# The last output chunk multiplied tile by tile, its first token tile scored and routed behind the second

## The reference: one block of a hybrid network with a mixture of experts

```python
h = rmsnorm(x, norm1_g)
u = h @ w_in
x = x + concatenate([y_a, y_b, y_c]) @ w_out          # the "mixed" rows y, 256 x 2048
h = rmsnorm(x, norm2_g)
pg = softmax(h @ rg_w + rg_b);  grp = argmax(pg)       # 4 groups
le = (h @ re_w + re_b)[experts of grp]                 # 8 experts a group
q, e = top_k(softmax(le), 2)                           # 2 experts a token
x = x + sum over the 2 experts of gate * (silu(h @ w_gate[e]) * (h @ w_up[e])) @ w_down[e]
out = rmsnorm(x, final_g)
```

## The kernel before

| tensor | before | multiple of 64? | after | multiple of 64? |
|---|---|---|---|---|
| `y_hi`, `y_lo` (stationary, output projection) | 193248, 209632 | no, 32 over | 193152, 209536 | yes |
| `h_both` (stationary in `rows()` for the values, moving in `channels()`) | 23488 | yes | 23552 | yes |
| `w_hi0`, `w_lo0` | 89024, 113600 | yes | 89088, 113664 | yes |
| `x_parts`, `pick` (sort) | 138176, 17536 | yes | 138240, 17536 | yes |
| `sorted_rows` | 193248 | no, 32 over | 193152 | yes |
| `iota_row`, `ones_b` | 189568, 191744 | yes | 189472, 191648 | no, 32 over |

## Time and profile before

### The profile page before, as it was taken

One profiled execution on the slowest core, in us unless ns is written; L12 is line 12 of the kernel. 1 busy time (PEld: TensorE's weight loads), 2 busy tenths in 40 slices (PEclk: granted clock), 3 DMA queues, 4 the chain that ended last, 5 costly groups with the idle time before them and its releaser, 6 DMA issues.

```text
span 1338.6 us, 15622 instructions
## 1 busy us (share of the span) xinstructions
PE 1237.3 (92%) x5882; PEld 645.0 (48%) x5882; DVE 555.5 (41%) x977; ACT 284.2 (21%) x390; POOL 6.0 (0%) x27
## 2 busy tenths in 40 slices
PE   5999999999999999999999898898989898998995
PEld 4888888888884333333333333333333333333332
DVE  5476888775555332323232222322322232232234
ACT  5343444464432001100010000001000000100002
POOL 1000000000000000000000000000000000000000
PEclk9999999999989999999999999999999999999998
DMA  7655455447468999999999999999999999999995
GB/s 270 214 175 198 143 182 179 163 157 301 170 251 333 424 427 427 428 428 429 428 428 429 429 428 428 429 428 428 429 428 427 429 429 428 428 429 428 423 423 238
DMA packets 65168, 471.74 MB, mean 352 GB/s; under 512 B 6087, under 2 KB 6599, under 8 KB 37868
## 3 DMA queue, kind: packets, MB, share of 16 engines
q1 hardware_dynamic: 65132, 471.24, 86.2%
HBM read 469.13 MB, written 2.10 MB: 352 GB/s over the span
## 4 chain that ended last, share of the span: by engine, by line
PE 58%; DMA 35%; DVE 3%; issue 2%; ACT 1%; SPq 0%; DVEq 0%; ACTq 0%
DMA ring<-in_w_up 29%; PE bank L1600 19%; PE bank L1403 10%; PE bank L1417 8%; PE bank L1635 7%; DMA zone_u<-in_w_up 5%; PE bank L1648 4%; PE bank L1418 4%; PE bank L1570 1%; PE bank L1601 1%; DVE zone_u L920 1%; PE bank L1529 1%; PE bank L1421 1%; DMA x_tok<-in_x 1%; ACT gatesT L787 0%
## 5 line engine op out<-in xcount | busy, mean ns | idle before, releaser
L1600 PE MATMUL bank<-ring,win 128*64 128x512 f32 x816 | 375.0, 614 | 46.2 <-DMA ring<-in_w_up 32.1
L1601 PE MATMUL bank<-ring,win 128*64 128x512 f32 x816 | 372.5, 610 | 0.0
L1600 PEld LDWEIGHTS bank<-ring,win 128*64 128x64 f32 x816 | 111.6, 141 | 289.1 <-issue 267.9
L1417 PE MATMUL bank<-h_both,w_hi 128*128 128x512 f32 x540 | 193.4, 400 | 0.3 <-DVE w_lo L383 0.3
L1251 DVE SCALAR_TENSOR_TENSOR x_tok<-bank,gate_of,x_tok 128x512 f32<-128x512 f32 x256 | 174.4, 744 | 25.0 <-PE bank L1648 24.0
L1635 PE MATMUL bank<-ring,hiddenT 128*64 128x512 f32 x704 | 157.6, 600 | 13.2 <-ACT gatesT L787 12.7
L383 DVE TENSOR_TENSOR w_lo<-stage,w_hi 128x2048 fp32r<-128x2048 f32 x60 | 137.4, 2296 | 74.9 <-ACT w_hi L377 74.9
L1418 PE MATMUL bank<-h_both,w_lo 128*128 128x256 f32 x540 | 151.8, 281 | 0.0
L377 ACT ACTIVATE w_hi<-stage 128x2048 fp32r<-128x2048 f32 x60 | 115.0, 1918 | 132.6 <-PE bank L1418 84.9
L779 ACT ACTIVATE rows_now<-bank,root_row 64x512 f32<-64x512 f32 x32 | 21.8, 680 | 566.6 <-PE bank L1601 566.6
L1648 PE MATMUL bank<-y_rows,gatesT 64*128 64x512 f32 x512 | 126.9, 615 | 1.0 <-DVE y_rows L1275 1.0
(11 more groups left out here) (239 smaller groups left out, 1014.0 us busy)
## 6 DMA issues: line engine op xcount, KB each, us to landing
ring<-in_w_gate SPq DMA_DIRECT2D x49, 2048.0 KB, 35.2
ring<-in_w_up SPq DMA_DIRECT2D x48, 2048.0 KB, 31.9
ring<-in_w_down SPq DMA_DIRECT2D x40, 2048.0 KB, 31.9
stage<-in_w_in SPq DMA_DIRECT2D x44, 1024.0 KB, 5.1
zone_u<-in_w_down SPq DMA_DIRECT2D x19, 2048.0 KB, 31.9
zone_u<-in_w_up SPq DMA_DIRECT2D x9, 2048.0 KB, 34.1
zone_u<-in_w_gate SPq DMA_DIRECT2D x9, 2048.0 KB, 35.4
stage<-in_w_out SPq DMA_DIRECT2D x16, 1024.0 KB, 5.0
```

The lines of the kernel that those rows point to most:

```text
L1417: M.matmul(banks[j][:, :], hi[:, at], both, start=(c == 0), stop=False)
L1600: M.matmul(bank[0][0:W_ROWS, :], rows_of[:, c, 0:W_ROWS], gate[:, at], start=(c == 0), stop=(c == C - 1))
L1601: ins = M.matmul(bank[0][UPPER, :], rows_of[:, c, 0:W_ROWS], up[:, at], start=(c == 0), stop=(c == C - 1))
```

## The change

Four things are changed. (a) In the last chunk of the last output block PE makes the twelve products of token tile 0 first and then those of tile 1, and signals tile 0 by a semaphore of its own (`mixed_first`); VectorE adds tile 0 at once, and PE turns tile 0 between the products of tile 1 (`by_tile`). (b) Tile 0 is scored right behind the products, then tile 1 is turned and scored; the transposes of tile 1 go half to bank 5, half to bank 4, and ScalarE and VectorE copy one half each. Mean, root and its inverse are made for each tile alone. (c) The routing steps are written for one tile each, and tile 0's stand before or between those of tile 1. A tile has two casts and one comparison less: the mask takes the index as it is and is added in the same instruction, and `index` holds the two choices side by side (`[P, T, 2, 33]`), so that PE makes twelve instead of six products for the places and four instead of two for the sums; KEEP_ROUTE falls from 30 to 20. (d) `root_of` and `masked` change places in memory, `below` goes and `root_row` is padded to 24 floats, which moves every tensor behind them (table above).

The diff, cut to its core (removed routing steps, which the list above shows, are left out):

```diff
-KEEP_ROUTE, KEEP_PICK = 30, 24
+KEEP_ROUTE, KEEP_PICK = 20, 24
...
-        masked = sb("masked", [P, T, E])
+        root_of = sb("root_of", [P, T, E + OVER])
...
-        below = sb("below", [P, T, E + 1])
-        index = sb("index", [P, T, E + 1], BF16)
+        index = sb("index", [P, T, 2, E + 1], BF16)
...
-        root_of = sb("root_of", [P, T, E + OVER])
-        root_row = sb("root_row", [P, 1])
+        masked = sb("masked", [P, T, E])
+        root_row = sb("root_row", [P, 24])[:, 0:1]
...
+            def root_of_tile(t):
+
+                act.wait_ge(mean_sq, 1 + t + 1)
+                nc.scalar.activation(RT_[:, t:t + 1], MS[:, t:t + 1], ACT.Sqrt).then_inc(root, 1)
+
             rows_hi(BLOCKS - 1, 0)
+            root_of_tile(0)
             turned_out(BLOCKS - 1)
             squares(BLOCKS - 1, 1)
-            act.wait_ge(mean_sq, 2)
-            nc.scalar.activation(RT_, MS, ACT.Sqrt).then_inc(root, 1)
+            act.wait_ge(x_turned, T * (BLOCKS - 1) + 2)
+            nc.scalar.activation(xT[:, 1, 0:NB // 2], bank[5][:, 0:NB // 2], ACT.Copy).then_inc(xT_half, 1)
+            root_of_tile(1)
             rows_hi(BLOCKS - 1, 1)
...
+            def add_tile(b, t):
+
+                at = x_tok[:, t, b * NB:(b + 1) * NB]
+                V.tensor_tensor(at, at, bank[MIXED_BANK[b % 2] + t][:, :], ALU.add).then_inc(mixed_added, 1)
...
-            add_mixed(BLOCKS - 1)
...
-            dve.wait_ge(sq_made, T * (BLOCKS - 2) + 1)
-            dve.wait_ge(mixed_added, T * (BLOCKS - 1) + 1)
-            last = x_tok[:, 0, (BLOCKS - 1) * NB:]
-            squared = did(V.scalar_tensor_tensor(sq_out[0], last, 1.0, last, ALU.mult, ALU.mult,
-                                                 accum_out=sq_parts[:, 0, BLOCKS - 1:BLOCKS]))
-            turned_out(BLOCKS - 1)
-            dve.wait_ge(sq_made, T * BLOCKS - 1)
-            after(squared)
-            after(did(V.tensor_reduce(SS, sq_parts[:, :, :], AX.X, ALU.add)))
-            V.tensor_scalar(MS, SS, 1.0 / D, EPS, ALU.mult, ALU.add).then_inc(mean_sq, 1)
-            dve.wait_ge(root, 2)
-            V.reciprocal(RSTD, RT_).then_inc(h_ready, 1)
-            dve.wait_ge(h_ready, T + 1)
...
+            def mean_of_tile(t):
+
+                after(did(V.tensor_reduce(SS[:, t:t + 1], sq_parts[:, t, :], AX.X, ALU.add)))
+                V.tensor_scalar(MS[:, t:t + 1], SS[:, t:t + 1], 1.0 / D, EPS, ALU.mult, ALU.add).then_inc(mean_sq, 1)
+
+            def root_of_tile(t):
+
+                dve.wait_ge(root, 1 + t + 1)
+                V.reciprocal(RSTD[:, t:t + 1], RT_[:, t:t + 1]).then_inc(h_ready, 1)
+
+            def logits_of(t):
+
+                dve.wait_ge(h_ready, T + t + 1)
+                dve.wait_ge(scored, T * LAST + t + 1)
+                return did(V.scalar_tensor_tensor(lg[:, t, :], bank[6 + t][:, 0:RW], RSTD[:, t:t + 1], rbias[:, :],
+                                                  ALU.mult, ALU.add))
...
+            def other_group(t):
+                return did(V.tensor_tensor(masked[:, t, :], grp_of[:, :], gidx[:, t, 0:1].broadcast_to([P, E]), ALU.not_equal))
+
+            def mask_others(t):
+                return did(V.scalar_tensor_tensor(masked[:, t, :], masked[:, t, :], MASKED, lg[:, t, GW:], ALU.mult, ALU.add))
...
+            def mark_later(t):
+
+                every = iota_row[:, 0:E + 1].unsqueeze(1).broadcast_to([P, 2, E + 1])
+                V.tensor_tensor(index[:, t, :, :], every, eidx[:, t, 0:2].unsqueeze(2).broadcast_to([P, 2, E + 1]),
+                                ALU.is_gt).then_inc(index_ready, 1)
...
+            dve.wait_ge(mixed_first, 1)
+            add_tile(LAST, 0)
+            dve.wait_ge(sq_made, T * (LAST - 1) + 1)
+            dve.wait_ge(mixed_added, T * LAST + 1)
+            last = x_tok[:, 0, LAST * NB:]
+            after(did(V.scalar_tensor_tensor(sq_out[0], last, 1.0, last, ALU.mult, ALU.mult, accum_out=sq_parts[:, 0, LAST:])))
+            mean_of_tile(0)
+            rows_lo(LAST, 0)
+            root_of_tile(0)
+            dve.wait_ge(used, chunk(4 * (OUT_BLOCK0 + LAST) + 3))
+            add_tile(LAST, 1)
...
+            a0 = logits_of(0)
+            dve.wait_ge(sq_made, T * BLOCKS - 1)
+            mean_of_tile(1)
+            after(a0)
+            a0 = group_max(0)
+            dve.wait_ge(x_turned, T * LAST + 3)
+            V.tensor_copy(xT[:, 1, NB // 2:], bank[4][:, NB // 2:]).then_inc(xT_dve, 1)
+            after(a0)
+            a0 = group_index(0)
+            root_of_tile(1)
+            after(a0)
+            a0 = other_group(0)
+            after(a0)
+            a0 = mask_others(0)
+            after(a0)
+            a0 = expert_max(0)
+            a1 = logits_of(1)
+            after(a1)
+            a1 = group_max(1)
+            a0 = expert_index(0)
+            after(a1)
+            a1 = group_index(1)
+            after(a1)
+            a1 = other_group(1)
+            mark_later(0)
+            after(a1)
+            a1 = mask_others(1)
+            after(a1)
+            a1 = expert_max(1)
+            after(a1)
+            a1 = expert_index(1)
+            after(a1)
+            mark_later(1)
...
+            chosen = did(V.tensor_copy(CHOICE.rearrange("p (t k) -> p t k", t=T), eidx[:, :, 0:2]))
...
-            rows_lo(BLOCKS - 1, 0)
+            after(chosen)
...
-            def rows(b, br, banks, left_hi, left_lo, before_chunk=None):
...
+                    if by_tile is None or m < STAGES - 1:
+                        order = [(i, t) for i in range(CM) for t in range(T)]
+                    else:
+                        order = [(i, t) for t in range(T) for i in range(CM)]
+                    for i, t in order:
+                        c, at, tt = m * CM + i, slice(i * NB, (i + 1) * NB), slice(t * P, (t + 1) * P)
+                        ins = products(banks[t][:, :], ((left_hi[:, c, tt], hi[:, at]), (left_hi[:, c, tt], lo[:, at]),
+                                                        (left_lo[:, c, tt], hi[:, at])), c == 0, c == C - 1)
+                        if by_tile is not None and m == STAGES - 1:
+                            by_tile(i, t, ins)
...
+            def turn_tile(b, t):
+
+                x_j = x_tok[:, t, b * NB:(b + 1) * NB].rearrange("p (k j) -> p j k", j=J)
+                pe.wait_ge(mixed_added, T * b + t + 1)
+                for j in range(J):
+                    other = b == BLOCKS - 1 and t == T - 1 and j >= 2
+                    ins = M.transpose(bank[4 if other else 4 + t][:, j * P:(j + 1) * P], x_j[:, j, :], ident[:, :])
+                    if b == BLOCKS - 1 and t == T - 1 and j == 1:
+                        ins.then_inc(x_turned, 1)
+                ins.then_inc(x_turned, 1)
...
+            def score_tile(b, t):
                 pe.wait_ge(rw_ready, RW_STEPS)
-                for t in range(T):
+                if b == BLOCKS - 1 and t == T - 1:
+                    pe.wait_ge(xT_half, 1)
+                else:
                     pe.wait_ge(xT_dve if t else xT_act, b + 1)
-                    for j in range(J):
-                        ins = M.matmul(bank[6 + t][:, 0:RW], xT[:, t, j * P:(j + 1) * P], rw[:, b * J + j, :],
-                                       start=(b == 0 and j == 0), stop=(b == BLOCKS - 1 and j == J - 1))
-                    ins.then_inc(scored, 1)
+                for j in range(J):
+                    if b == BLOCKS - 1 and t == T - 1 and j == 2:
+                        pe.wait_ge(xT_dve, b + 1)
+                    ins = M.matmul(bank[6 + t][:, 0:RW], xT[:, t, j * P:(j + 1) * P], rw[:, b * J + j, :],
+                                   start=(b == 0 and j == 0), stop=(b == BLOCKS - 1 and j == J - 1))
+                ins.then_inc(scored, 1)
...
+            def first_tile_out(i, t, ins):
+
+                if t == 0 and i == CM - 1:
+                    ins.then_inc(mixed_first, 1)
+                if t == 1 and i == 1:
+                    turn_tile(BLOCKS - 1, 0)
...
-            turn_block(BLOCKS - 1)
-            score_block(BLOCKS - 1)
+                rows(b, b % 3, bank[at:at + 2], yT_hi, yT_lo, former_block if i else mixers_done,
+                     first_tile_out if i == BLOCKS - 1 else None)
+
+            score_tile(BLOCKS - 1, 0)
+            turn_tile(BLOCKS - 1, 1)
+            score_tile(BLOCKS - 1, 1)
...
-                later = index[:, t, 1:]
-                M.matmul(dst, before_b[:, :], later, start=True, stop=False)
-                M.matmul(dst, from_b[:, :], index[:, t, 0:E], start=False, stop=False)
-                other = index[:, 1, 0:E] if t == 0 else index[:, 0, 1:]
-                M.matmul(dst, ones_b[:, :], other, start=False, stop=True).then_inc(places_done, 1)
+                for k in range(2):
+                    M.matmul(dst, before_b[:, :], index[:, t, k, 1:], start=(k == 0), stop=False)
+                    M.matmul(dst, from_b[:, :], index[:, t, k, 0:E], start=False, stop=False)
```

(22 more changed lines are left out.)

63 lines of the change are left out of this document (16 added, 47 removed).

## The result

| | before | after |
|---|---|---|
| median, us | 1338.49 (1337.86 to 1338.9) | 1329.69 (1329.44 to 1330.13, 4 runs) |
| ratio to before | | 0.9932, 95% interval 0.992 to 0.9944 |
| the profiled execution, its span | 1340.45, 1338.6 | 1329.68, 1327.9 |

The direction was right, 3.6 us of gain were not foreseen, and the two terms of the sum did not come out alike: the tail won 3.4 us in the profile where 2.8 were forecast, the products 0.4 where 2.4 were.

The account below looks back on a forecast made before the run. The kernel was taken as bound by a DMA transfer of fixed length whose start PE's progress to the sort sets. 2.4 (spacing) + 2.8 (tail) = 5.2 us won, giving 1333.3 us, range 1330.9 to 1336.2.

Parts of the forecast that it names:

- the tail: Last output block up to the sort: reordered tiles and shorter routing steps win 2.8 us, bounds 1.4 and 3.9.
- the products: Output projection: operand starts at a multiple of 64 bytes bring 384 products from 233 to 227 ns, 2.4 us.
- The full stream: Expert loads, 414.60 to 1320.60 us: fixed length, 906 us at DMA share 1.00; only its start can move.
- Rival 1: Output projection: spacing stays at 233 ns, operand start not the cause, only 2.8 won; 1335.7 us, chance 0.25.
- rival 3: All PE stages: spacing depends on operands' places to each other, channels() and values lose; 1341.0 us, chance 0.06.
- rival 4: All PE stages: same dependence the other way, all reach the short spacing, 4.1 us more; 1329.2 us, chance 0.07.
- P: End of all products of the last block before the change, 387.12 us, from which later times are counted.
- the working at the full clock: Last products to sort: 2.1 + 0.68 + 0.5 = 3.3 us won, sort at P + 7.95 instead of P + 11.24.
- us to spare: Last chunk: VectorE's 3.1 us on tile 0 fit within 3.3 us of tile 1's products, 0.2 to spare.
- logits of tile 1: Routing after the last block: VectorE has them within 3.1 us of the last product.
- the DMA's pause: Ahead of the sort's first half piece: the 3.1 us gap closes, no gap of over 1 us left.
- The 0.5 charged for the clock: Between last products and sort: 0.5 us taken off the 3.3 won, in case PE's waits lower the clock.

Follow-up runs that it names:

- the last but one experiment: Kernel before with 224 bytes of padding ahead of pos, so y_hi and w_hi starts differ by a multiple of 256; 1336.5 us, ratio 0.9978.
- the table of pairs: Kernel of products alone, no loads or reference work, 20 series with both operands' starts varied modulo 256; 226.7 to 234.3 ns a product.
- the kernel without fillers: Kernel after with KEEP_ROUTE and KEEP_PICK at 0, leaving out 44 products that nobody reads; 1332.29 us, ratio 0.9953.

## Why the prediction was wrong

**The full stream.** This is the step that failed: "a transfer of fixed length, and no engine can shorten it. What can move is its start", and for the profile after "906 us at a DMA share of 1.00 unchanged". The change moves the ring from 23488 to 23552, and the stream's length depends on that: 6.6 us in the profile, 5.3 to 7.1 in the profiles of three other pairs of kernels and 6.3 to 7.5 in their medians. The table of starts showed the new place of `h_both`, and `ring0` begins where `h_both` does; I asked of each start only what it does to PE. A DMA share of 1.00 says that the queue is never empty, not that each packet is as short as it can be: between 420 and 1300 us a packet of 16 KB took 615.1 ns in the mean before and 611.3 after (the medians, 613 and 611, show only half of this). The Trainium skill had the rule that asks for this: "DMA: Bandwidth & Descriptors", section "How a descriptor splits into AXI transactions", says that a transfer that does not start at a multiple of 256 bytes begins its first transaction at the boundary below and pays for the bytes it does not use. It is written of reads; the runs here show that a multiple of 256 counts at the side where the ring is written. Its account of the cost does not fit them: an estimate from that page, 65 transactions for 64 in a row of 16 KB, is 1.6%, two to three times the 0.5 to 0.7% measured, and with the bytes before the start as the cost 32 over would be the cheapest of the places off the multiple, where it was the slowest (428.1 GB/s). So the runs show the condition, and the mechanism behind it stays open.

**The spacing of the products.** The step said of the values' and the output's products that "the two differ in little else" than in whether the start is a multiple of 64, and took 2.4 us between bounds of 0 and 2.4. Measured: 0.4. The size was right for an operand well placed (2.3 in the last but one experiment), but the multiple of 64 is not the condition. Before, `y_hi` stood 32 from `w_hi` modulo 256, the values' operand 0, and `x_parts` 64 from `pick`. After, they stand at 128, 0 and 128. Measured are 233.3, 226.8 and 233.3 ns before and 232.4, 226.8 and 232.4 after, each within 0.2 of what the table of pairs has for that distance. The sort's 233 ns, named as evidence against and then set aside, was the row to follow: an aligned operand with the long spacing refuted the condition. Rival 1 had the size of this term and rival 3 its cause ("their places to each other"); `channels()` and the values lost nothing, and there both operands moved by the same 64 bytes. That rival 4's time, 1329.2, lies within 0.5 us of the measured one is chance: the shorter stages on which it rests did not come, and `channels()` kept its 159.6 us.

**The tail.** Right. The sort starts at 7.81 us behind the end of the products of this stage, counted without the transposes as P was, where the working at the full clock had 7.95. Its parts hold too: 0.26 us to spare (0.2), logits of tile 1 at 3.05 behind the last product (3.1), `mine` 0.47 behind the end of `index` (0.47), the DMA's pause closed. The 0.5 charged for the clock was not due, since it did not fall; the kernel without fillers shows that the charge was not idle. A third of the 3.4 is no shorter path: 1.15 is what the low clock had cost before, and it did not fall after. The working had part of this in it, as it took the scores at their length at the full clock.

**Why the total was off.** Forecast 5.2 = 2.4 + 2.8. Measured in the profiles: 0.4 + 3.4 + 6.6 + 0.3 of the rest. Two errors, -2.0 and +0.6, and one term that was missing. Without the missing term the time would have been inside the range in spite of both errors: the kernel whose tail alone is new is 2.9 us faster than before, which from 1338.5 is 1335.6.

## What to carry to other kernels

When a change moves tensors, list every start modulo 256 before and after, and ask of each what reads and what writes it: the targets of long loads first, since a kernel bound by its DMA pays there for the whole stream. A DMA share of 1.00 is no fixed length as long as the packet's own time can change. And where one row refutes the condition that a term rests on, the term is to be taken at that row's size, not at the size of the rows that fit.

## What the runs showed of the hardware

- Loads of 16 KB a partition into slots at a multiple of 256 bytes run at 431.3 GB/s and elsewhere at 428.1 to 429.3, with nothing else running; in the kernel 429 and 426.
- fp32r products 128x512 with a weight load each are 226.7 to 227.6 ns apart if both operands start at the same place modulo 256 (and at a multiple of 32), and up to 234.3 ns otherwise, 3%. Against 226.7 a difference of 192 costs 2.3 ns, 128 costs 5.8, 64 and odd multiples of 32 cost 6.6 or more. The duration of one in the profile shows it as well: 389 or 390, 393 and 396 ns at a distance of 0, 128 and 32. Only distances and starts as in the table were tried, for this one form; why the distance counts is not shown.
- A tail of the same length ran once at a clock of 0.50 and once at 1.00, with products that ended 2.5 us earlier as the only difference: 1.15 us in 11.65. Whether the clock falls in a gap of this length does not follow from the gap alone in these runs, and what else decides stays open.
